# U activations of sixteen dense tokens by fetched expert rows, beside the one-hot products

## The reference, cut to what matters

```python
u = jnp.take(U, ic, axis=0)
act = jax.nn.gelu(jnp.einsum('chkd,cd->chk', u, xc), approximate=False)
vv = jnp.take(V, ic, axis=0)
return jnp.einsum('chk,chkd->cd', gc * act, vv)
```

## Time and profile before

| | |
|---|---|
| median of 3 runs | 1821.33 us (1820.68 to 1823.36) |
| profiled execution | 1820.24 us |
| its span | 1818.5 us |
| PE, matmuls busy | 1750.3 us (96%) |
| PE, weight loads busy | 1546.9 us (85%) |
| DVE busy | 1413.8 us (78%) |
| ACT busy | 694.9 us (38%) |
| POOL busy | 559.6 us (31%) |
| DMA | 435.31 MB, mean 239 GB/s |

### The profile page before, as it was taken

One profiled execution on the slowest core, in us unless ns is written; L12 is line 12 of the kernel. 1 busy time (PEld: TensorE's weight loads), 2 busy tenths in 40 slices (PEclk: granted clock), 3 DMA queues, 4 the chain that ended last, 5 costly groups with the idle time before them and its releaser, 6 DMA issues.

```text
span 1818.5 us, 36541 instructions
## 1 busy us (share of the span) xinstructions
PE 1750.3 (96%) x12342; PEld 1546.9 (85%) x12342; DVE 1413.8 (78%) x2912; ACT 694.9 (38%) x1301; POOL 559.6 (31%) x449
## 2 busy tenths in 40 slices
PE   3999899999999999999999999999999999999996
PEld 3776788847899999999999999999888888888885
DVE  5895666556878878888888888677698888888887
ACT  3333454415344344433333333333343333333331
POOL 6011522103345343533322332353133323333210
PEclk9999999999999999999999999999999999999998
DMA  9751000064333333698889888999899999999981
GB/s 313 255 172 48 2 3 3 26 235 174 119 130 113 119 130 124 224 310 281 289 295 326 283 285 295 316 394 388 339 408 352 353 351 355 357 351 351 352 284 70
DMA packets 245066, 435.31 MB, mean 239 GB/s; under 512 B 84898, under 2 KB 157956, under 8 KB 244996
## 3 DMA queue, kind: packets, MB, share of 16 engines
q1 hardware_dynamic: 207968, 300.07, 47.7%
q0 software_dynamic: 36864, 134.23, 20.0%
q10 hardware_dynamic: 164, 0.05, 0.0%
HBM read 379.77 MB, written 54.53 MB: 239 GB/s over the span
## 4 chain that ended last, share of the span: by engine, by line
PE 76%; DVE 2%; ACT 0%; another core or an unknown queue 0%; issue 0%; ACTq 0%; DVEq 0%
PE bank L1460 29%; PE bank L1969 9%; PE bank L1967 9%; PE bank L1968 9%; PE bank L1440 6%; PE bank L1897 5%; PE bank L1950 5%; PE bank L1404 2%; PE bank L1909 1%; DVE n_stats L1370 0%; DVE wide L1384 0%; DVE wide L2367 0%; DVE wide L1379 0%; DVE wide L2366 0%; PE bank L1852 0%
## 5 line engine op out<-in xcount | busy, mean ns | idle before, releaser
L1460 PE MATMUL bank<-hh,uh 128*128 128x384 f32 x1024 | 357.1, 349 | 0.0
L1460 PE MATMUL bank<-hl,uh 128*128 128x384 f32 x1024 | 343.1, 335 | 0.0
L1967 PE MATMUL bank<-vh,wh 128*128 128x512 f32 x768 | 298.8, 389 | 3.1 <-DVE wl L2327 3.1
L1968 PE MATMUL bank<-vl,wh 128*128 128x512 f32 x768 | 298.8, 389 | 0.0
L1969 PE MATMUL bank<-vh,wl 128*128 128x512 f32 x768 | 298.8, 389 | 0.0
L1518 POOL DMA_INDIRECT vsel<-in_peer_v,picks x128 | 149.7, 1170 | 418.5 <-DVE gt L1544 404.2
L2101 ACT ACTIVATE vh<-vraw 128x1024 fp32r<-128x1024 f32 x128 | 135.9, 1062 | 286.3 <-PE bank L1969 271.2
L2324 DVE TENSOR_TENSOR vl<-vraw,vh 128x1024 fp32r<-128x1024 f32 x128 | 156.5, 1223 | 81.5 <-ACT vh L2101 81.5
L1518 POOL DMA_INDIRECT wide<-in_peer_u,picks x108 | 147.2, 1363 | 233.3 <-DVE wide L1525 220.3
L1460 PE MATMUL bank<-hh,ul 128*128 128x384 f32 x1024 | 198.9, 335 | 0.0
L1460 PEld LDWEIGHTS bank<-hl,uh 128*128 128x128 f32 x1024 | 193.0, 188 | 0.0
(11 more groups left out here) (345 smaller groups left out, 2963.1 us busy)
## 6 DMA issues: line engine op xcount, KB each, us to landing
urows<-in_peer_u SPq DMA_DIRECT2D x128, 512.0 KB
vraw<-in_peer_v SPq DMA_DIRECT2D x128, 512.0 KB, 6.5
scored<-act_out SPq DMA_DIRECT2D x128, 192.0 KB
gates<-SS SPq DMA_DIRECT2D x16, 1536.0 KB
gtile<-gates SPq DMA_DIRECT2D x32, 768.0 KB
act_in<-scored SPq DMA_DIRECT2D x128, 192.0 KB, 6.6
wt<-in_w_in SPq DMA_DIRECT2D x19, 512.0 KB, 4.5
wq<-in_peer_wq SPq DMA_DIRECT2D x18, 512.0 KB, 3.8
```

Of the source, the lines that this page charges most:

```text
L1460: last = pe.matmul(bank, u[:, k, :], h[:, k, 0:TD], start=(n == 0), stop=(n == 3 * KD - 1))
L1967: pe.matmul(b, wh[s][:, cols], vh[s][:, half], start=first, stop=False)
L1968: pe.matmul(b, wh[s][:, cols], vl[s][:, half], start=False, stop=False)
```

## The change

The last 16 (`EXTRA`) of the 384 dense tokens, 368 to 383, no longer take part in the U products: these have 368 (`TU`) columns. Their activations are computed from fetched rows, as for the picked tokens, but with 16 tokens x 8 heads on the 128 partitions, so that one fetch and one dot handle eight picks of each of the 16 tokens; 16 such fetches and dots make all 128 picks. Two are done in each of turns 0 and 1, one in each of turns 2 to 13 (`XPAIRS`, `XTURNS`), the first in s = 1 of VectorE, the second in s = 2. Their buffers are `usel[3]` and `vsel[3]`. For this `hx` holds the 16 token rows eight times (TensorE turns them in group 0, ScalarE copies them, seven DMAs repeat them), `xrows` the expert numbers of the picks, by eight DMAs that ScalarE issues at the start of turn 0.

In turn 13 ScalarE applies Gelu to the 16 sums of each partition; in turn 14 VectorE makes a block matrix of them, one small product of TensorE brings them to the layout of `turned[2]`, and VectorE multiplies the shares of the 16 tokens by them. What is spread for these tokens in turn 15 is thus share times activation, and the columns 368 to 383 of `act_out` are set to 1.0 once, so the V phase stays as it is. Turns 14 and 15 are written out on TensorE and VectorE, turns 12 to 15 on ScalarE. Three semaphores of the softmax are joined in one.

```diff
+EXTRA = 16
+TU = TD - EXTRA
+XPAIRS = 2
+XTURNS = EXTRA - XPAIRS
...
-            last = pe.matmul(bank, u[:, k, :], h[:, k, 0:TD], start=(n == 0), stop=(n == 3 * KD - 1))
+            last = pe.matmul(bank, u[:, k, :], h[:, k, 0:TU], start=(n == 0), stop=(n == 3 * KD - 1))
...
-        act.activation(self.out[:, s, :], self.banks[s % 2][:, 0:TD], ACT.Gelu).then_inc(self.gelu_up, 1)
+        act.activation(self.out[:, s, 0:TU], self.banks[s % 2][:, 0:TU], ACT.Gelu).then_inc(self.gelu_up, 1)
...
             for i in range(BLOCKS):
                 fetched(0, 3, 3 * i, 3)
+                for e in range((i < XTURNS) + (i < XPAIRS)):
+                    if i == 0 and e == 0:
+                        pool.wait_ge(xrows_in, START + 16 * (2 * HEADS - 1))
+                        pool.wait_ge(scores.ul_up, START + 4 * SPREAD + 1)
+                    elif i:
+                        pool.wait_ge(xdot_up, START + min(i + 2, 2 * i - 1) + e)
+                    f = 2 * i + e if i < XPAIRS else i + XPAIRS
+                    pool.indirect_dma_start(out=xbuf[e][:, :], out_offset=None, in_=sel.rows[0],
+                                            in_offset=bass.IndirectOffsetOnAxis(ap=xrows[:, f:f + 1], axis=0))\
+                        .then_inc(xrow_in[e], 16)
...
+            for j in range(2):
+                for k in range(4):
+                    last = pe.transpose(banks[4 + j][0:EXTRA, k * P:(k + 1) * P], h2[:, 4 * j + k, TU:TD], ident[:, :])
+                last.then_inc(ht_up, 1)
...
+                    if s == 3 and xsum:
+                        pe.wait_ge(xact_up, START + XBLOCK)
+                        pe.matmul(banks[7][:, 0:EXTRA], xblock[:, :], of_token[:, :], start=True, stop=True)\
+                            .then_inc(xact_up, 1)
...
+            for j in range(2):
+                act.wait_ge(ht_up, START + j + 3)
+                act.activation(hx[0:EXTRA, 512 * j:512 * j + 512], banks[4 + j][0:EXTRA, :], ACT.Copy)\
+                    .then_inc(ht_out, 1)
+            act.wait_ge(ht_out, START + 4)
+            for h in range(1, HEADS):
+                act.dma_start(hx[EXTRA * h:EXTRA * (h + 1), :], hx[0:EXTRA, :]).then_inc(xrows_in, 16)
...
+            act.wait_ge(picks_up, START + 2)
+            for h in range(HEADS):
+                act.dma_start(xrows[EXTRA * h:EXTRA * (h + 1), :],
+                              xpicks[P - EXTRA:P, TOPK * h:TOPK * (h + 1)]).then_inc(xrows_in, 16)
...
+                        if xlast and o and s == 2:
+                            act.wait_ge(xdot_up, START + EXTRA)
+                            act.activation(xgel, xdots, ACT.Gelu).then_inc(xact_up, 1)
...
             dve.memset(ones[:, :], 1.0).then_inc(ones_up, 1)
+            dve.memset(act_out[:, :, TU:TD], 1.0)
...
+            dve.scalar_tensor_tensor(out=xpicks[:, :], in0=IS[:, NT - 2, :, :].rearrange("p h k -> p (h k)"),
+                                     scalar=float(NKEYS), in1=JS[:, NT - 2, :, :].rearrange("p h k -> p (h k)"),
+                                     op0=ALU.mult, op1=ALU.add).then_inc(picks_up, 1)
+            dve.tensor_reduce(of_row[:, :], ident[:, :].rearrange("p (h t) -> p h t", t=EXTRA), AX.X, ALU.add)
+            dve.tensor_reduce(of_token[:, :], ident[:, :].rearrange("p (h t) -> p t h", t=EXTRA), AX.X, ALU.add)
...
+            def extra_dot(e, t, f):
+
+                dve.wait_ge(xrow_in[e], 16 * t + 16)
+                dve.scalar_tensor_tensor(out=xbuf[e][:, :], in0=xbuf[e][:, :], scalar=1.0, in1=hx[:, :],
+                                         op0=ALU.mult, op1=ALU.mult, accum_out=xdots[:, bass.ds(f, 1)])\
+                    .then_inc(xdot_up, 1)
...
+                    if s == 0 and xsum:
+                        dve.wait_ge(xact_up, START + XGEL)
+                        dve.tensor_tensor(xblock[:, :].rearrange("p (h k) -> p h k", k=TOPK),
+                                          xgel.unsqueeze(1).broadcast_to([P, HEADS, TOPK]),
+                                          of_row[:, :].unsqueeze(2).broadcast_to([P, HEADS, TOPK]), ALU.mult)\
+                            .then_inc(xact_up, 1)
...
                     elif s == 1:
                         sel.dot(dve, 2, t)
+                        if extra:
+                            extra_dot(0, t, t + XPAIRS if extra == 1 else 2 * t)
                     elif s == 2:
                         sel.weigh(dve, 0, 3, 3 * t, t)
                         sel.add(dve, 0, t, 3 * t)
+                        if extra == 2:
+                            extra_dot(1, t, 2 * t + 1)
...
+            with dve.Fori(SPREAD, SPREAD + XPAIRS) as i:
+                spread_turn(i, 2)
+            with dve.Fori(SPREAD + XPAIRS, SPREAD + XTURNS) as i:
+                spread_turn(i, 1)
+            spread_turn(SPREAD + XTURNS, 0, True)
+            dve.wait_ge(xact_up, START + XSUM)
+            dve.tensor_tensor(turned[2][:, TU:TD], turned[2][:, TU:TD], banks[7][:, 0:EXTRA], ALU.mult)\
+                .then_inc(xact_up, 1)
+            dve.wait_ge(xact_up, START + XSHARE)
+            spread_turn(SPREAD + XTURNS + 1, 0)
```

More of the change, by code:

```diff
@@ L1580, in emit_experts, with extra @@
         v["late"].close()
+        def extra(name, width, dt=F32):
+            return ctx.enter_context(nc.sbuf_tensor(name, [P, width], dt, side="right"))
+        hx, xgate, xblock = extra("hx", D), extra("xgate", 2 * EXTRA), extra("xblock", P)
+        xpicks, xrows = extra("xpicks", P, U32), extra("xrows", EXTRA, U32)
+        of_row, of_token = extra("of_row", HEADS), extra("of_token", EXTRA)
+        xdots, xgel = xgate[:, 0:EXTRA], xgate[:, EXTRA:]
         def rt(name, shape, dt=F32):
@@ L1636, in emit_experts @@
         ht_up, ht_out, picks_up = sem("ht_up"), sem("ht_out"), sem("picks_up")
+        xrows_in, xdot_up, xact_up = (sem(n) for n in ("xrows_in", "xdot_up", "xact_up"))
+        XGEL, XBLOCK, XSUM, XSHARE = 1, 2, 3, 4
+        xbuf, xrow_in = [usel[3], vsel[3]], [sel.us_in[3], sel.vs_in[3]]
         wq_in = [sem(f"wq_in{c}") for c in range(2)]
@@ L1952, in _ @@
                         last.then_inc(spread, 1)
+            with pe.Fori(SPREAD, SPREAD + XTURNS) as i:
+                spread_turn(i)
+            for i in range(SPREAD + XTURNS, CLEAR):
+                spread_turn(i, i == SPREAD + XTURNS)
             with pe.Fori(CLEAR, LAST) as i:
@@ L2089, in _ @@
                                 .then_inc(staged, 1)
+                        if xlast and o and s == 2:
+                            act.wait_ge(xdot_up, START + EXTRA)
+                            act.activation(xgel, xdots, ACT.Gelu).then_inc(xact_up, 1)
                         scores.gelu(act, i, s)
+            with act.Fori(0, XTURNS // 2 - 1) as b:
+                spread_turns(b)
+            for b in range(XTURNS // 2 - 1, BLOCKS // 2):
+                spread_turns(b, b == XTURNS // 2 - 1)
             with act.Fori(CLEAR, LAST) as i:
@@ L2278, in following, with spread_turn @@
                     scores.late_remainder(dve, i + 1, 0)
-            with dve.Fori(SPREAD, CLEAR) as i:
+            def extra_dot(e, t, f):
[3 more added lines that the diff above has]
+                    .then_inc(xdot_up, 1)
+            def spread_turn(i, extra, xsum=False):
                 t = i - SPREAD
@@ L2331, in group @@
                 first = 2 - 2 * q
[L2332 removed]
+                before = [BLOCKS + LAST - CLEAR] * 3 + [XTURNS + LAST - CLEAR]
+                before_v = [BLOCKS + LAST - CLEAR] * 3 + [XPAIRS + LAST - CLEAR]
                 done = 2 * g + (SECOND - 2)
@@ L2341, in group @@
                         sel.weigh(dve, first, 2, done, g + (BLOCKS + LAST - CLEAR - 1))
-                        sel.add(dve, first, pair + before[first], done)
+                        sel.add(dve, first, pair + before_v[first], done)
                     elif s == 3:
-                        sel.add(dve, first + 1, pair + before[first + 1], done + 1)
+                        sel.add(dve, first + 1, pair + before_v[first + 1], done + 1)
             for s in range(4):
```

54 lines of the change are left out of this document (28 added, 26 removed).

## The result

The changed kernel takes 1805.14 us (median of 5 runs, 1801.97 to 1807.78). Measured beside it, the kernel before took 1821.33 us (1817.04 to 1824.13): a ratio of 0.9911, 95% interval 0.9893 to 0.993, so 16.2 us faster, with 12.7 to 19.5 by the interval. The forecast was 1803.7.

What follows compares the result with a forecast made beforehand. The prediction took TensorE to be bound by the columns streaming through its matmuls. Less 20.5 us, plus 1.1, 0.3 and 1.5, made 17.6 us less than the median 1821.33: 1803.7, range 1799.5 to 1811.

Steps and rivals of the forecast that it cites:

- the additions: All costs added beside the narrowing, on TensorE and by turn 0's stall: 2.9 us.
- The columns: U phase: each of 3,072 matmuls loses 16 of 384 columns, 6.6 to 6.7 ns each, 20.5 us less.
- TensorE's additions: Eight transposes in group 0 (0.9 us at most), a small product in turn 14 (0.2), written-out turns (0.3).
- VectorE in the steady turns: Turns 2 to 13: one extra dot of 1.2 us fits the slack, 1.4 us remain, so it costs nothing.
- Turns with two dots: Turns 0 and 1: two extra dots fit VectorE's slack, with 0.2 us remaining.
- The fetch in the steady turns: Spreading turns: the extra fetch lands about 7.28 us after issue, in time by 1.8 us; DMA share about 0.96.
- The turning point: Spreading turns: a landing more than 10.6 us after the start of issue stalls TensorE in each of 15 turns.
- Turn 0: the mis-sized term: Turn 0: the first extra fetch lands late and TensorE stalls 1.5 us, once; bounds 0 and 3.
- ScalarE's eight issues: Before turn 0's first `evacuate`: DMA issues of 0.32 us each, 2.8 us in all, costed at nothing.
- The weights: Rival, U products: weight loads set the pace, 368 columns keep 384's distance, only costs remain: 1824.2 us; chance 0.05.
- A late fetch in every turn: Rival, spreading: extra rows reach VectorE late each turn; 1811 us at some 0.5 a turn, 1826 at 1.5 beyond; chance 0.09.
- Late blocks behind the spreading: Rival: the five turns there are bound by the DMA, 3.2 us of gain lost, 1807 to 1809; chance 0.08.

Runs made afterwards that it cites:

- experiment 1: The kernel before with U products and Gelu narrowed to 368 columns, activations of tokens 368 to 383 left out: 1801.48 us, ratio 0.9892.
- 3: The kernel before with U products and Gelu narrowed to 320 columns, tokens 320 to 383 left out, a single run: 1755.01 us.
- experiment 11: The changed kernel with two more unused reductions of 128 x 1,024 on VectorE behind each extra dot, a single run: 1827.57 us.
- 5: The changed kernel with no extra pick in turn 0, two each in turns 1 to 3, one in each of 4 to 13: 1804.44 us, ratio 0.9917.
- 8: The changed kernel with no extra pick in turns 0 and 1, one in 2 to 9, two in 10 to 13: 1803.98 us, ratio 0.9912.
- 10: The changed kernel with two extra fetches in each of turns 0 to 13, 12 of them used by nobody, a single run: 1815.68 us.
- experiment 2: The changed kernel with its U products at 384 columns again, so the additions alone: 1824.33 us, ratio 1.0017.
- experiment 12: The changed kernel with one pick in each of turns 0 to 11, two in 12 and 13, turn 0's dot moved behind s = 3's adds: 1801.35 us, ratio 0.9886.
- experiment 6: The changed kernel with the eight small copies issued by SyncE before its last store of group 9, instead of by ScalarE: 1801.35 us, ratio 0.9907.
- experiment 7: As experiment 6, with TensorE's first-block transposes and half its product moved before the waits that end the routing: 1807.83 us, ratio 0.9934.

## Why the prediction was right, and where its sizes were off

**The direction and the time.** 1803.7 forecast, 1805.14 measured. By the medians the parts agree as well: the narrowing gave 19.7 us (16.6 to 22.6) for 20.5, the additions took 3.1 (1.3 to 4.9) for 2.9. In the profiled executions both parts are larger than forecast, 23 us of gain and about 9 of losses, and mostly cancel, so the closeness of the total was in part luck. So was the closeness of the 19.7: in its trace, too, the columns give 23, and a slow stretch of the clock, late blocks behind the spreading and a longer V phase take back 4.5.

**The columns.** Right in mechanism. The distance went from 173.6 to 166.4 ns (750.36 to 752.69, 14 distances in 2.33 us) where I had 166.9, 7.2 ns for 16 columns, give or take 1 ns of rounding. The size was off: a block outside the spreading went from 5.05 to 4.88 us, 7.1 ns a matmul for my 6.6 to 6.7, and a turn from 25.60 to 24.84, 0.76 where I had 0.64. So the traces' gross gain is about 23 us for my 20.5: 64 blocks by 0.17 and 64 by 0.19. Why a block of the spreading gives 0.19 and not 0.17 stays open. By the rule of the Trainium skill (TensorE: Matmul & The Clock Gate, Back-to-back issue gap) that load and matmul both set the distance, it would have been 2.1 ns, an estimate from that page's figures; experiments 1 and 3 speak against that. My remark that the trace before has no width but multiples of 64 was wrong in two small places (one matmul of 98 columns, 64 of one column); these few would not have shown a rounding.

**TensorE's additions.** The eight narrow transposes cost 0.87 us, as the 0.9 said:

```profile
448.17 1.03 PE L1911 MATMUL bank<-ident,wide 128*128 128x128 f32 x8
449.04 1.04 PE L1915 MATMUL bank<-ident,wide 128*16 128x128 f32 x8
449.91 1.04 PE L1447 MATMUL bank<-ident,urows 128*128 128x128 f32 x8
```

Fewer loaded columns don't help. The small product cost 0.23 us in turn 14, as the 0.2 said, and the written-out turns nothing, for my 0.3:

```profile
1116.81 0.29 PE L1975 MATMUL bank<-of_token,xblock 128*128 128x16 f32 x2
```

**VectorE in the steady turns.** Right: the extra dot costs nothing in turns 2 to 13, and experiment 11 shows that it would have, had it taken some 1.4 us more. Turns with two dots: I gave them 0.2 us of slack on VectorE; the runs show a cost of 0.4 to 1.75 us, from late U rows.

**The fetch in the steady turns.** It cost nothing there, as forecast, and the DMA share is 0.93 and not 0.96; but the landing was mis-sized. Where VectorE waited it was 8.87 to 9.04 us, not 7.28, so the 1.8 us by which I had it in time were not there, and the lead of 1.5 us at q = 3 covered the rest. The turning point that I gave, a landing of 10.6 us, was not reached. What I had wrong is who pays first with more load. The rival said that the extra rows come late to VectorE. Experiments 5, 8 and 10 show that SyncE's U rows come late to TensorE first, at about 1 us a turn, because SyncE issues them behind two stores. The edge is one 512 KB fetch away.

**Turn 0: the mis-sized term.** I had 1.5 us (0 to 3) for the extra fetch and 0 for ScalarE's eight issues. The trace of the changed kernel has 4.75 us for the pause with the slow clock behind it, 1.6 for the slow clock at the start and 1.5 in turn 1. Three steps of mine failed. The issues: 5.03 us for eight, 0.63 each, where I took 0.32 from a row of another shape and looked only at who waits for ScalarE, not at GpSimd, which waits for the copies, nor at the 5 us that the last of them took to land. So the fetch started 9.5 us into turn 0 (750.33 less 740.87), where my 754.24 was 6.8 us into it (the turn began at 747.45 before). The landing: 7.62 us for 7.28. Together the row came 3.0 us later in the turn than I had it, and TensorE, slowed at the turn's start, came 1.7 us later than I had it (757.96 less 740.87, for 15.4): my pause of 1.5 thus became 2.9. And a pause of TensorE costs more than its length, if the clock falls behind it; my sum had no such term. The 3.2 us that I estimated from the Trainium skill (DMA: Bandwidth & Descriptors, Anatomy of one DMA) for such a fetch is not what any trace shows at this load: where VectorE waited for the row it was 7.4 to 9.1 us in turn 0 and 8.7 to 9.6 in later turns.

**The rivals.** The weights don't set the pace (1, 3). A late fetch in every turn did not come about. Late blocks behind the spreading cost the changed kernel 0.5 us and experiment 1 3.6, but the kernel before has 1.5 of them. So this rival is real in some executions, and against the kernel before it took 2.1 us of the gain in experiment 1, less than my 3.2.

**What stays open.** How much of turn 0's cost is there in each execution. Each kernel has one trace. The changed kernel's shows about 9 us of losses beside the gain, of which the 1.6 us of slow clock at the start are not the additions' (experiment 1 has them too). By the runs of experiment 2 the additions cost only 3.1 us, and the changed kernel's runs are spread over 6 us. Executions without the slow clock would account for part of that. It was not shown, since the other runs have no trace.

## What to carry to other kernels

A fetch that is hidden in a steady loop is not hidden in the loop's first turn. It did not take longer there (7.62 us for 8.93 in a middle turn), it was issued later: 9.5 us into turn 0, behind six other fetches and the copies, where a middle turn issues it 2.1 us into the turn (875.06 less 872.97). Place its consumer behind the burst (experiment 12), rather than issuing it earlier into a queue that is still busy (6, 7). Where a shared DMA is near full, ask which queue is late first; it need not be the one that you add to, and look whether its transfers are slower or only issued later. Price a stall of TensorE with the clock that may be lost behind it, and the issue of a DMA by a row of the same shape.

## What the runs showed of the hardware

Two pauses of 0.8 to 1.0 us within 2 us of each other, after hundreds of microseconds of full work, were followed by a stretch of 3.4 us at 1.2 GHz in nine of the twelve profiled executions that have them, and not in the other three: the kernel before, experiment 6 and experiment 12. The price was 1.6 us each time. The distance of the matmuls was then 307 ns for 166.4 at 368 columns. Longer pauses in the spreading went both ways too: of nine pauses between 1.94 and 2.91 us, the clock fell at seven and stayed up at two, 2.55 us (experiment 6) and 2.83 (experiment 7).

A DMA share of 0.93 over ten turns left TensorE next to no wait, 0.96 to 0.97 did not; that holds for these turns, since behind the spreading the kernel before ran at 1.01 with TensorE busy in 109.30 of 110 us. A store's issue on SyncE's queue, behind a store of 1.5 MB, lasted 4.3 to 13.7 us in the spreading of the traces with additions.
